# MLP by Strassen's scheme, in two phases with u in DRAM, and h normed ahead of its transposes

## The reference

```python
h = h + mixed @ w_out[i]
hn = rms_norm(h, g_mlp[i])
h = h + jnp.square(jax.nn.relu(hn @ w_up[i])) @ w_down[i]     # w_up 1024 x 4096, w_down 4096 x 1024
gate = jax.nn.sigmoid(rms_norm(h, g_ple[i]) @ w_ple_gate[i])
h = h + gate * (p[i] @ w_ple_proj[i])
```

## Time and profile before

| | |
|---|---|
| median of 3 runs | 3375.0 us (3373.9 to 3375.9) |
| the profiled execution | 3371.46 us, its span 3369.4 us |
| PE busy | 3288.0 us, 98% of the span |
| DVE, ACT, POOL busy | 1650.3, 1239.7, 846.4 us |
| first `e_up_acc` matmul, last `e_down_acc` matmul | 1727.9 us, 3122.8 us |

### The profile page before, as it was taken

How to read it: one execution, slowest core, us unless ns; L and a number is a source line. 1 busy time by engine, 2 the same in 40 slices (tenths; PEclk the granted TensorE clock), 3 DMA queues, 4 the chain that set the end, 5 groups by cost and what they waited for, 6 DMA issues and landing times.

```text
span 3369.4 us, 49728 instructions
## 1 busy us (share of the span) xinstructions
PE 3288.0 (98%) x18272; PEld 2833.2 (84%) x18272; DVE 1650.3 (49%) x3005; ACT 1239.7 (37%) x2269; POOL 846.4 (25%) x767
## 2 busy tenths in 40 slices
PE   8999999999999999998999999999999999999998
PEld 8988888888888899996888888888888888888887
DVE  5133344888888856655643333333533333333332
ACT  4011112777777777861222222211211112122432
POOL 2133330111111166742222222212122222222322
PEclk9999999999999999998999999999999999999999
DMA  5233337003032258746851111111521111112221
GB/s 178 80 113 115 125 125 181 26 27 83 20 83 54 61 115 204 181 121 200 255 211 50 50 40 47 50 50 50 185 80 50 49 38 49 50 50 81 91 85 54
DMA packets 248803, 316.46 MB, mean 94 GB/s; under 512 B 74416, under 2 KB 187440, under 8 KB 243376
## 3 DMA queue, kind: packets, MB, share of 16 engines
q1 hardware_dynamic: 245280, 307.82, 30.5%
q10 hardware_dynamic: 3344, 6.29, 0.7%
HBM read 221.39 MB, written 92.67 MB: 93 GB/s over the span
## 4 chain that ended last, share of the span: by engine, by line
PE 90%; DVE 5%; issue 1%; POOL 1%; DMA 1%; SPq 1%; ACT 1%; POOLq 0%; DVEq 0%
PE e_up_acc L138 7%; PE e_up_acc L140 7%; PE e_up_acc L139 7%; PE e_down_acc L140 7%; PE e_down_acc L138 7%; PE e_down_acc L139 7%; PE a_acc L140 5%; PE a_acc L139 5%; PE a_acc L138 5%; PE c_pv L846 5%; PE b_pv L986 4%; PE c_turned L835 3%; PE c_scores L827 3%; PE c_scores L828 3%; DVE c_neg_half L743 2%; DVE c_a_row L776 2%
## 5 line engine op out<-in xcount | busy, mean ns | idle before, releaser
L1887 DVE SCALAR_TENSOR_TENSOR e_h<-e_down_acc,g_inv,e_h 128x512 f32<-128x512 f32 x512 | 378.4, 749 | 814.6 <-PE e_down_acc L140 814.3
L138 PE MATMUL e_up_acc<-e_xt_hi,e_up_hi 128*128 128x512 f32 x1024 | 398.7, 389 | 0.0
L138 PE MATMUL e_down_acc<-e_down_hi,e_u_hi 128*128 128x512 f32 x1024 | 398.4, 389 | 0.0
L140 PE MATMUL e_up_acc<-e_xt_hi,e_up_lo 128*128 128x512 f32 x1024 | 398.4, 389 | 0.0
L140 PE MATMUL e_down_acc<-e_down_hi,e_u_lo 128*128 128x512 f32 x1024 | 398.4, 389 | 0.0
L139 PE MATMUL e_up_acc<-e_xt_lo,e_up_hi 128*128 128x512 f32 x1024 | 398.3, 389 | 0.0
L139 PE MATMUL e_down_acc<-e_down_lo,e_u_hi 128*128 128x512 f32 x1024 | 398.3, 389 | 0.0
L1906 POOL TENSOR_TENSOR e_sq<-e_r 128x512 f32<-128x512 f32 x128 | 134.8, 1053 | 1009.4 <-ACT e_r L1856 1009.4
L743 DVE TENSOR_REDUCE c_neg_half<-c_scores 128x1 f32<-128x1024 f32 x256 | 313.1, 1223 | 82.4 <-PE c_scores L828 82.4
L700 ACT ACTIVATE c_e<-c_scores,c_neg_max 128x1024 f32<-128x1024 f32 x256 | 287.1, 1121 | 58.1 <-DVE c_neg_max L750 50.0
L846 PE MATMUL c_pv<-c_v,c_at 128*128 128x128 f32 x2048 | 270.1, 275 | 0.4 <-ACT c_o L714 0.4
(11 more groups left out here) (168 smaller groups left out, 6674.3 us busy)
## 6 DMA issues: line engine op xcount, KB each, us to landing
s_qkt<-a_hl SPq DMA_DIRECT2D x128, 256.0 KB, 2.8
e_up_raw<-w_up_dram SPq DMA_DIRECT2D x32, 1024.0 KB, 5.3
e_down_raw<-w_down_dram SPq DMA_DIRECT2D x32, 1024.0 KB, 4.9
b_kt<-s_qkt SPq DMA_DIRECT2D x64, 256.0 KB, 9.3
a_w_raw<-w_in_dram SPq DMA_DIRECT2D x24, 512.0 KB, 5.3
d_nd<-s_nd SPq DMA_DIRECT2D x48, 256.0 KB, 3.1
b_qs<-s_qkt SPq DMA_DIRECT2D x32, 256.0 KB, 5.2
s_nd<-b_nout SPq DMA_DIRECT2D x16, 512.0 KB, 4.3
```

The source lines that it names most:

```text
L138: nc.tensor.matmul(out, lhs_hi, rhs_hi, start=first, stop=False)
L140: return nc.tensor.matmul(out, lhs_lo, rhs_hi, start=False, stop=last)
L1887: nc.vector.scalar_tensor_tensor(out=tile, in0=self.down_acc[:, k % 4], scalar=self.fixed.inv[:, z * HT + t:z * HT + t + 1], in1=tile, op0 ...
```

## The change

`Mlp` is replaced by two classes. Both use Strassen's scheme in Winograd's form on 2x2 blocks: 7 block products (q = 0 to 6) in place of 8, with sums of the blocks made ahead and partial results combined behind.

**`Up`** has 32 steps (2 halves of the tokens by 16 blocks of 256 hidden columns). A step has 7 products of 12 matmuls. POOL makes 4 sums of weight blocks (`sum_a`, `sum_s4`), each 128x512; ACT and DVE split 7 weight operands (`hi_a`, `lo_a`). The token operands (`b_hi`, `b_lo`, 7 of 128x2048) stay for 16 steps and are made anew at the switch to the second half, with 4 sums, 3 of them on POOL. Two PSUM banks are read out by ACT when a product is done, and the next product is accumulated on top (`onto=True`). ACT, then DVE, make `u` (4 tiles of 128x512 a step), and SP stores it in DRAM.

**`Down`** has 32 passes (2 halves by 8 groups of 512 hidden columns by 2 sets of 4 token tiles). A pass has 14 products of 6 matmuls, 7 for each of two token pairs s. Per pass SP loads 2 tiles of `u`, POOL makes 8 sums of 128x2x128 (`sum_u`), ACT splits 128x1792 twice (`hi_u`), DVE makes its rest twice (`lo_u`), and DVE adds a 128x512 bank to `h` after each product (14 `add`). Per group, so for two passes, POOL makes 4 sums of the weights of 128x1024 (`sum_w`) and 4 of the 7 rests of them, and DVE the other 3 (`lo_w`).

In `Mix`, `h` is now multiplied by its norm's factor (POOL raises to -1/2 in `root`, ACT multiplies in `scale`) before PE transposes it, so that `inv` is gone. The last two tiles' products with `w_out` are split in halves of the contraction. `Gate` has other places in memory, loads its weights later and splits them otherwise. Nothing is in an engine's loop any more.

The core of the diff:

```diff
-def matmul3(nc, out, lhs_hi, lhs_lo, rhs_hi, rhs_lo, first, last):
+def matmul3(nc, out, lhs_hi, lhs_lo, rhs_hi, rhs_lo, first, last, onto=False):
...
     def turn_h(self, pe, t):
         nc, S = self.nc, self.S
-        pe.wait_ge(S["h"], 2 * t + 2)
+        pe.wait_ge(S["hn"], t + 1)
...
+class Up:
+    def sum_a(self, pool, n):
+        pool.wait_ge(S["a_in"], 32 * n + 32)
+        nc.gpsimd.tensor_tensor(a[:, :, 4], a[:, :, 1], a[:, :, 3], ALU.add).then_inc(S["a_sum"], 1)
...
+            for n in range(STEPS):
+                if n + 1 < STEPS:
+                    self.load_a(sp, n + 1)
...
+class Down:
+    def sum_w(self, pool, g):
+        nc.gpsimd.tensor_tensor(w[:, 4], w[:, 1], w[:, 0], ALU.subtract).then_inc(S["w_sum"], 1)
...
+    def lo_w(self, eng, op, g, q, sem):
+        S, s = self.S, g % 2
+        eng.wait_ge(S["w_hi"], 7 * g + q + 1)
+        op(self.w_lo[s][:, q], self.w_raw[s][:, q], self.w_hi[s][:, q].bitcast(F32), ALU.subtract).then_inc(S[sem], 1)
...
+    def sum_u(self, pool, m):
+        nc.gpsimd.tensor_tensor(u[:, :, 4], u[:, :, 1], u[:, :, 3], ALU.add).then_inc(S["u_sum"], 1)
...
+        @block.vector
+            def add(k, q, s):
...
+                dve.wait_ge(S["prod"], 14 * k + 2 * q + s + 1)
...
+                nc.vector.tensor_tensor(tile, bank[:], tile, ALU.add).then_inc(S["h"], 1)
...
+        @block.gpsimd
+        def _(pool):
+            for k in range(DPS):
+                g = k // 2
+                for m in (2 * k + 2, 2 * k + 3):
+                    if m < 2 * DPS:
+                        self.sum_u(pool, m)
+                if g + 1 < GROUPS:
+                    if k % 2 == 0:
+                        self.sum_w(pool, g + 1)
+                    else:
+                        for q in range(3, Q):
+                            self.lo_w(pool, nc.gpsimd.tensor_tensor, g + 1, q, "w_lop")
...
+        @block.tensor
+            def product(k, q, s):
...
+                if q in (2, 3, 4):
+                    self.wait_sums(pe, k, q - 2, s)
...
+                if q == 6:
+                    self.wait_sums(pe, k, 4, s)
```

More of the change, by code:

```diff
@@ L1386, in program, with root @@
+    def root(self, pool, t):
+        S, v = self.S, slice(t % 2, t % 2 + 1)
+        pool.wait_ge(S["mean"], t + 1)
+        if t >= 2:
+            pool.wait_ge(S["hn"], t - 1)
+        self.nc.gpsimd.tensor_tensor(self.rstd[:, v], self.mean[:, v], self.fixed.half[:], ALU.pow).then_inc(S["rstd"], 1)
+    def program(self, block, dilated, up):
         nc, D, S, fixed = self.nc, self.D, self.S, self.fixed
@@ L1481, in _ @@
                     weigh(t + 2)
[L1482 to L1487, removed]
+                if t:
+                    self.scale(act, t - 1)
+                if t == TILES - 3:
+                    up.hi_b(act, 0, 0)
+                if t == TILES - 2:
+                    up.hi_b(act, 0, 1)
+                    for q in range(3):
+                        up.hi_a(act, 0, q)
+                    up.hi_b(act, 0, 2)
+                if t < TILES - 1:
+                    self.square(act, t)
+            up.hi_b(act, 0, 3)
         @block.vector
@@ L1658, in _ @@
             self.turn_h(pe, 0)
[L1659 to L1662, removed]
+            for t in range(2, TILES - 2):
+                turn(t + 1, 0)
+                turn(t + 1, 1)
                 for g in range(G):
@@ new lines, in wait_sums, with load_early, begin_scalar @@
+    def wait_sums(self, eng, k, q, s):
+        eng.wait_ge(self.S["h"], 14 * k + 2 * q + s + 1)
+    def load_early(self, sp):
+        up = self.up
+        up.wait_parts(sp)
+        self.load_u(sp, 0)
+        up.wait_product(sp, 2)
+        self.load_u(sp, 1)
+        up.wait_product(sp, 3)
+        for t in range(4):
+            self.load_h(sp, 0, t)
+    def begin_scalar(self, act, part):
+        if part == 0:
+            for q in range(3):
+                self.hi_w(act, 0, q)
+        elif part == 1:
+            self.hi_u(act, 0)
+        else:
+            for q in range(3, self.Q):
+                self.hi_w(act, 0, q)
+            self.hi_u(act, 1)
@@ new lines, in begin_vector, with begin_pool, program @@
+    def begin_vector(self, dve, part):
+        if part == 0:
+            for q in range(3):
+                self.lo_w(dve, self.nc.vector.tensor_tensor, 0, q, "w_lo")
+            self.lo_u(dve, 0)
+        else:
+            self.lo_u(dve, 1)
+    def begin_pool(self, pool):
+        self.sum_u(pool, 0)
+        self.sum_u(pool, 1)
+        for q in range(3, self.Q):
+            self.lo_w(pool, self.nc.gpsimd.tensor_tensor, 0, q, "w_lop")
+    def program(self, block, gate):
+        nc, S, Q, up = self.nc, self.S, self.Q, self.up
+        FG, GROUPS, DPS, HT = self.FG, self.GROUPS, self.DPS, self.HT
@@ new lines, in _ @@
+            for k in range(DPS):
+                g = k // 2
+                for q in range(Q):
+                    for s in range(2):
+                        add(k, q, s)
+                    if q in (1, 4):
+                        m = 2 * k + 2 + q // 4
+                        if m < 2 * DPS:
+                            self.lo_u(dve, m)
+                    if k % 2 and g + 1 < GROUPS and q in (2, 3, 5):
+                        self.lo_w(dve, nc.vector.tensor_tensor, g + 1, q - 2 - q // 5, "w_lo")
@@ L1946, in step, with __init__ @@
+            for k in range(DPS):
+                for q in range(Q):
+                    for s in range(2):
+                        product(k, q, s)
+                    if k == DPS - 1 and q == 4:
                         gate.turn(pe, 0)
-            self.blocks(pe, step)
 class Gate:
-    def __init__(self, kit, fixed, mlp):
-        self.nc, self.D, self.fixed, self.mlp = kit.nc, kit.dram, fixed, mlp
+    def __init__(self, kit, fixed, down):
+        self.nc, self.D, self.fixed, self.down = kit.nc, kit.dram, fixed, down
```

1099 lines of the change are left out of this document (699 added, 400 removed).

## The result

The changed kernel takes 3419.4 us as a median (3412.0 to 3421.6), the kernel before, run beside it, 3374.5 us: a ratio of 1.013 (95% interval 1.0112 to 1.0147), so 45 us and 1.3% slower. The profiled execution took 3421.6 us, 50.4 us of span more than the one before.

The account below looks back on a forecast made before the run. PE, busy for 98% of the span, was taken as the bound. The terms -174 + 130 + 24 + 50 + 2 + 8 = +40 gave 3414 us, 1.2% slower; range 3368 to 3455 us, leaving out 2 in 10.

Parts of the forecast that it names:

- -174 for 768 matmuls: `Up` and `Down`: 5376 matmuls in place of 6144 save 174 us, if PE never waits.
- Two passes of `Down`, +130: POOL and DVE exclude each other on SBUF operands: 46.2 us per two passes against PE's 38.1, 16 times, +130 us.
- the fourth rival: `Down`: a `sum_u` costs 1.0 us in place of 0.73, +69 us, 3480 us; chance 0.07.
- hand-overs: `Down`: some ten turns between POOL and DVE per two passes, each taking 0.14 us off.
- what the semaphores give back: `Down`: semaphores between POOL's dependent sums give back about as much time as some ten turns of 0.14 us take off.
- the hole: `Down`, odd pass: POOL's `lo_w` of q = 3 waits 5.9 us for ACT's halves; 3.5 us more per two passes.
- the third rival: Turns as forecast, but gap filled, short sums cheaper or end waits halved: 3350 to 3368 us; 0.15 including everything up to forecast.
- The ends of `Down`, +24: PE waits 13 us at the start of `Down`; the switch of the halves adds 11 us; together +24.
- `Up`, +50: Waits in `Up`: step 0 +15, switch of halves +16, `sum_w(0)` +4, last step +2, transposes +2, slow clock +11.
- the low clock: `Up`: PE runs at half clock after waits; +8 us for three such waits, +3 for lesser ones.
- `Mix` +2, `Gate` +8: `Mix`: a lag for the first tile, +2 us; `Gate`: POOL's 8 rests of weights and later loads, +8 us.
- The second rival: The port matters little, DVE and POOL overlap: -97 us, 3278 us; chance 0.08.

Follow-up runs that it names:

- x1_psum: Changed kernel with DVE's rests of u and w in `Down` read from PSUM instead of SBUF, from the second group on; 3329.9 us.
- x5_more: Changed kernel with POOL making the last of its four sums of w twice from group 1 on; 3444.8 us.
- x6_more_psum: The kernel of x1_psum with POOL making the last of its four sums of w twice from group 1 on; 3337.8 us.
- x7_four: Changed kernel with another order of work in `Down`; still four rests of w on POOL and three on DVE; 3346.7 us.
- x2_early: Changed kernel with ACT's halves of w parted over both passes, q = 3 to 6 made at the end of the even pass; 3391.9 us.
- x4_share_ends: Changed kernel with `Down` reordered, five rests of w on DVE and two on POOL, and three issues on SP moved; 3286.3 us.

## Why the prediction was right, step by step

The side and the size were right: 3414 us predicted, 3419.4 measured. That the two are so close is in part luck, since two passes of `Down` cost 12 us less than predicted and its ends 13 us more. By its terms (profiled executions, 40 us predicted and 50.4 measured):

- **-174 for 768 matmuls:** right; between waits they follow each other at 0.2266 us.
- **Two passes of `Down`, +130:** measured 16 x (45.5 - 38.1) = +118. The mechanism is the one that the rows of before showed (x1_psum, x5_more, x6_more_psum). The Trainium skill (SBUF — State Buffer, Who interferes with whom) also says that a DVE instruction with at most one SBUF input does not contend with GpSimd, outside of DVE's 2-port modes; x1_psum agrees, with 2.02 us for `lo_u` and 2.46 for POOL's `lo_w`. `sum_u` was the operation without a row: 0.73 us estimated, 0.73 measured, so the fourth rival (1.0 us) is out. The sum came to 46.2 us, the trace has 45.5. POOL's wait for ACT was 5.6 us (5.9 summed), there are 11 hand-overs and not ten (44 in the four times two passes up to 2652.1 us, counted as in x7_four), and POOL waits 0.65 us for loads; 42.8 + 3.5 - 1.5 + 0.65 make 45.4. So the term that was too large is, as far as this sum goes, what the semaphores give back, put at 1.4. What the prediction did not see is that the loads of `u` wait next, once the hole is filled: x2_early comes to 43.3 us, where the third rival had 42.8, and this kernel does not fill the hole.
- **The ends of `Down`, +24:** 155.3 - 118 = +37. The start waits 12.2 us (13 predicted), but by luck: square, store, load, sums, half and rest as I listed them are 13.8 us and a square against the 11 us that PE has, which does not give 13. In the trace the last square of `Up` begins only 4 us after `Down`'s first product and takes 2.9 us, and the load of `u` takes 7.8 us, not 4. At the switch I counted +11 over what was saved elsewhere. PE waits 12.2 and 15.0 us there, and starts 12 matmuls in the 5 us behind each, at a granted clock of 0.50. The four passes around the switch take 118.2 us where four others take 91, so it is +27. Each wait hangs on a store of `h` that lands after 5.2 and 6.8 us and on the load of `u` issued behind it, 6.5 and 6.0 us; I had summed bytes instead. This is the term that was most too small. A low clock I had put at nothing within the passes; it shows there too, though not behind each wait of 3.1 us (22 matmuls at 1.00 behind the one that ends at 2470.1 us). How much of it is on the path is not shown. Behind the one that ends at 2515.6 us (columns as in the earlier trace rows):

```profile
2515.00:2520.00 5.00, 4.37 (x12) 3.50 (x13) 2.97 (x5) 1.69 (x1) 4.92 (x3) 0.66 0.00 0
```

- **`Up`, +50:** +55.8. Step 0 waits 15.4 us for `e_u` (15 predicted; in its chain stands a turn that I did not count, a square of DVE's held up by a rest of POOL's, 4.35 us in place of 0.69), the switch 1.6 + 10.6 + 3.6 = 15.8 us (16), `sum_w(0)` makes 2.8 + 0.8 us (4), the last step 2.1 (2), the transposes of tile 15 wait 3.7 and some 0.6 around them (2). The rest, some 13 us, is what I had put at 11 for the low clock. In the last 5 us of the wait of step 0 the granted clock is half, and in the 5 us behind it 0.67, with 14 matmuls where the next 5 us have 24 (columns as in the earlier trace rows):

```profile
1767.00:1772.00 5.00, 0.00 (x0) 0.00 (x0) 2.60 (x3) 2.00 (x4) 4.07 (x3) 0.50 0.00 1
1772.00:1777.00 5.00, 4.55 (x14) 3.70 (x15) 4.69 (x8) 1.54 (x4) 0.08 (x1) 0.67 0.14 54
1777.00:1782.00 5.00, 5.00 (x24) 4.13 (x23) 2.00 (x2) 1.62 (x3) 1.21 (x1) 1.00 0.46 155
```

- **`Mix` +2, `Gate` +8:** `Mix`'s first transposes stand 3.2 us later than before, in phases that the change does not touch; 2.9 us are `Mix`'s own, with new waits of 6.7 us for `hn` of the first tile and of 1.5 us for `hn` just ahead of `Up`, while two waits of before are gone. `Gate` takes 10.1 us more; 4.5 of them are PE's wait for DVE's `f_xt_lo`. DVE itself waits 2.4 us of that time for ACT's `f_xt_hi`, which stands behind ACT's halves of the gate's weights; POOL's rests of the weights, which I had named, are not what PE waits for there.
- **The second rival** (the port matters little, 3278 us) is refuted for this kernel, but its time is within reach: x4_share_ends takes 3286 us with every operation of the scheme in it. Its turns, 40.3 us less 15 or 16 hand-overs of 0.14 us, come to PE's 38.1 us, and two passes take 38.8 us; 31.5 us of the gain came from SP's order.

What stays open: how much of the 72.7 us between x7_four and the changed kernel belongs to which place in the order (only the hole was tried alone), and what the hole costs by itself.

## What to carry to other kernels

When work moves from the bound engine to DVE and POOL, add up what both do on SBUF operands as if it were one engine (POOL's instructions and DVE's with two SBUF inputs), and compare that sum with the bound, not each engine's busy time. If the sum is over, a subtraction costs half as much of it on DVE as on POOL (1.22 against 2.42 us for 1024 columns), and one operand in PSUM takes it out altogether. Then look at what DVE must wait for ahead of the instructions that free PE's banks: their order was worth 73 us here, the shares 29. And when one wait is closed, look for the one that opens: without the hole POOL waited 4.6 us for loads.

## What the runs showed of the hardware

- A long instruction of POOL makes even a short one of DVE long: at 1754.28 us the `scalar_tensor_tensor` of 512 columns with `e_u` as both inputs took 4.35 us behind a rest of POOL's that took 4.88 and ended 0.55 us before it did; its mean in `Up` is 0.96 us, where the addition from PSUM beside it has 0.69. Here, reading the same tile twice counted as two SBUF operands.
- ACT is outside of all this: `h_u_hi` takes 1.70 us on average and `h_w_hi` 1.05, in the changed kernel as in x1_psum, where POOL and DVE no longer hinder each other.
- POOL's short sums start every 0.70 us though each is shown with 0.74, and a dependent one 0.82 us after the one that it needs (2481.93, 2482.75, 2483.45 us). The price per sum by the line of long ones held down to 256 columns: 0.73 us.
